# One edit to a one-core transformer kernel: bias tables in four column groups, sums spread between products, first weight units in halves

## What is computed

```python
xn = rms_norm(h, g)                      # before each product; sums of squares over 1024 channels
h = h + rms_norm(ffn, g_ffn_post)        # the end of the first FFN
h = h + sigmoid(h @ w_ple_gate) * e      # starts on the h above, without a norm
bias = rel_bias[t5_bucket(distance)]     # 33 x 16 values, wanted for 1680 distances
logit = q @ k + bias                     # in the last layer, long after the tables are made
```

## Time and profile before

| what | value |
|---|---|
| median of three runs | 1934.17 us (1933.32 to 1936.07) |
| the profiled execution's own time | 1936.29 us |
| its span in the trace | 1934.5 us |
| PE busy | 1891.3 us of it (98%) |
| DVE, ACT, POOL busy | 983.0, 761.2, 763.3 us |
| granted clock of PE, mean | 0.987 of full speed |

### The profile page before, as it was taken

One profiled execution on the slowest core, in us unless ns is written; L12 is line 12 of the kernel. 1 busy time (PEld: TensorE's weight loads), 2 busy tenths in 40 slices (PEclk: granted clock), 3 DMA queues, 4 the chain that ended last, 5 costly groups with the idle time before them and its releaser, 6 DMA issues.

```text
span 1934.5 us, 25284 instructions
## 1 busy us (share of the span) xinstructions
PE 1891.3 (98%) x9354; PEld 1545.6 (80%) x9354; DVE 983.0 (51%) x1639; ACT 761.2 (39%) x1307; POOL 763.3 (39%) x325
## 2 busy tenths in 40 slices
PE   7988999999999999999999999999999999999998
PEld 6886688888888788888888888898866688888886
DVE  6767367643344544235444333743688444344444
ACT  6786544322223351233222222423599642222221
POOL 4323043543444334454445444356300135445452
PEclk9998999999999899999999999999999999999999
DMA  5212032332323223973323333234112023323321
GB/s 190 66 45 66 19 102 69 114 105 87 103 86 103 67 83 108 164 194 100 99 97 97 106 101 95 79 100 136 39 34 67 21 80 118 98 87 97 98 91 62
DMA packets 52238, 177.55 MB, mean 92 GB/s; under 512 B 5527, under 2 KB 5911, under 8 KB 52152
## 3 DMA queue, kind: packets, MB, share of 16 engines
q1 hardware_dynamic: 47952, 166.22, 27.1%
q10 hardware_dynamic: 4200, 10.15, 3.5%
HBM read 166.88 MB, written 9.47 MB: 91 GB/s over the span
## 4 chain that ended last, share of the span: by engine, by line
PE 89%; DVE 6%; ACT 4%; issue 1%; DMA 0%; ACTq 0%; DVEq 0%
PE ps L422 27%; PE ps L423 27%; PE ps L424 27%; PE ps L907 2%; ACT arena L1112 2%; PE ps L893 1%; DVE arena L2263 1%; DVE arena L2240 1%; PE ps L930 1%; DVE arena L1651 1%; ACT arena L1069 1%; PE ps L608 1%; PE ps L574 1%; PE ps L579 1%; PE ps L592 1%
## 5 line engine op out<-in xcount | busy, mean ns | idle before, releaser
L383 POOL TENSOR_TENSOR WL<-raw,WH 128x1024 fp32r<-128x1024 f32 x295 | 736.2, 2510 | 1103.6 <-ACT WH L994 1103.4
L422 PE MATMUL ps<-XH,WH 128*128 128x512 f32 (+1 forms) x1280 | 497.5, 389 | 10.6 <-DMA ident<-in_ident 10.6
L994 ACT ACTIVATE WH<-raw 128x1024 fp32r<-128x1024 f32 x295 | 304.4, 1053 | 509.6 <-PE ps L424 461.0
L423 PE MATMUL ps<-XL,WH 128*128 128x512 f32 (+1 forms) x1280 | 495.8, 387 | 0.0
L424 PE MATMUL ps<-XH,WL 128*128 128x512 f32 (+1 forms) x1280 | 495.6, 387 | 0.0
L422 PE MATMUL ps<-HH,WH 128*128 128x512 f32 x1080 | 423.6, 392 | 5.3 <-DVE XL L1784 4.5
L424 PE MATMUL ps<-HH,WL 128*128 128x512 f32 x1080 | 421.4, 390 | 0.0
L423 PE MATMUL ps<-HL,WH 128*128 128x512 f32 x1080 | 421.2, 390 | 0.0
L422 PEld LDWEIGHTS ps<-XH,WH 128*128 128x128 f32 x1280 | 243.0, 190 | 59.6 <-issue 11.4
L424 PEld LDWEIGHTS ps<-XH,WL 128*128 128x128 f32 x1280 | 242.8, 190 | 48.0
L423 PEld LDWEIGHTS ps<-XL,WH 128*128 128x128 f32 x1280 | 243.0, 190 | 47.2
(11 more groups left out here) (260 smaller groups left out, 1715.0 us busy)
## 6 DMA issues: line engine op xcount, KB each, us to landing
raw<-in_weights SPq DMA_DIRECT2D x301, 512.0 KB, 3.6
tab<-arena ACTq DMA_DIRECT2D x1, 5120.0 KB, 76.7
arena<-tab SPq DMA_DIRECT2D x16, 256.0 KB, 2.9
ftab<-arena ACTq DMA_DIRECT2D x1, 2080.0 KB, 23.4
h<-in_xT SPq DMA_DIRECT2D x8, 256.0 KB, 8.8
out_T<-h SPq DMA_DIRECT2D x8, 256.0 KB, 2.1
arena<-ftab ACTq DMA_DIRECT2D x4, 256.0 KB
arena<-in_pT ACTq DMA_DIRECT2D x1, 512.0 KB, 3.5
```

The lines of the kernel that those rows point to most:

```text
L383: nc.gpsimd.tensor_tensor(WL[:, s, :], raw[:, s, :], WH[:, s, :].bitcast(f32), SUB)\
L422: nc.tensor.matmul(out, wh, xh, start=start, stop=False)
L423: nc.tensor.matmul(out, wh, xl, start=False, stop=False)
L994: nc.scalar.activation(WH[:, s, :], raw[:, s, :], ACT.Copy).then_inc(*m["whi"].tick())
```

## The change

In the opening, units 0 and 1 are loaded, rounded and lowered in halves of 512 columns, the identity comes second on ScalarE's queue, positions and mask are issued after the norm's first part, ScalarE loads its table ahead of the data, and PE runs twelve products of `ones` before `quad`, which no longer waits for `vec` and `ident` itself. At the FFN's opening the sum of squares is cut in three and set between products. At the tables, `spread` comes first, then the four pieces, each into its own 32 columns of the array and its own 32 partitions of one bank, then eight products of the identity. The table rows therefore lie on partitions 0, 32, 64 and 96 onward, and are stored in five transfers in place of two. VectorE's order in the update of h is changed so that XL of a chunk comes one operation earlier.

```diff
         @block.sync
         def _(sp):
-            for c in range(DC):
-                if c in (0, 1, 4, 5):
-                    at = c // 4 * 2 + c % 2
-                    sp.dma_start(raw[:, at, :], io["weights"][SOURCE[at]]).then_inc(raw_in[at], 16)
+            def unit(at, half=None):
+                cols = slice(0, 1024) if half is None else slice(512 * half, 512 * half + 512)
+                sp.dma_start(raw[:, at, cols], io["weights"][SOURCE[at]][:, cols])\
+                  .then_inc(half_in[at] if half == 0 else raw_in[at], 16)
+            def chunk(c):
                 sp.dma_start(h[:, c, :], io["xT"][c * P:(c + 1) * P, :]).then_inc(x_in[c], 16)
+            unit(0, 0)
+            chunk(0)
+            unit(1, 0)
+            chunk(1)
+            unit(0, 1)
+            unit(1, 1)
+            for c in range(2, DC):
+                if c in (4, 5):
+                    unit(c - 2)
+                chunk(c)
...
-            sp.wait_ge(sems["tab_st"], 32)
+            sp.wait_ge(sems["tab_st"], 80)
...
-            for u in range(20):
+            def lower_half(u, half):
+                cols = slice(512 * half, 512 * half + 512)
+                pool.wait_ge(*((sems["whi"], u + 1) if half else (sems["first_hi"], u + 1)))
+                nc.gpsimd.tensor_tensor(WL[:, u, cols], raw[:, u, cols], WH[:, u, cols].bitcast(f32), SUB)\
+                  .then_inc(sems["wlo" if half else "first_lo"], 1)
+            for half in range(2):
+                for u in range(2):
+                    lower_half(u, half)
+            for u in range(2, 20):
...
-                        if c % 4 == 0 and t % 2 == 0:
+                        if halves and c < 4:
+                            if t % 2 == 0 and c % 2 == 0:
+                                pe.wait_ge(sems["wlo" if c else "first_lo"], u + 1)
+                        elif c % 4 == 0 and t % 2 == 0:
...
-            def tables(part):
-                for i in part:
-                    if i == 3:
-                        pe.wait_ge(*m["tab_out"].next())
-                    w = min(S, 1680 - S * i)
-                    nc.tensor.matmul(ps[0:H2, 4 + i % 3, 0:w], relb[0:33, 0:H2], ohs[0:33, S * i:S * i + w],
-                                     start=True, stop=True).then_inc(*m["tab_done"].tick())
+            def tables():
+                pe.wait_ge(sems["onehot_in"], 16)
+                pe.wait_ge(sems["relb_in"], 16)
+                pe.wait_ge(sems["relb_pad"], 1)
+                for i in range(4):
+                    cols, w = piece(i)
+                    last = nc.tensor.matmul(ps[32 * i:32 * i + 32, 4, 0:w], relb[0:33, :], ohs[0:33, cols],
+                                            start=True, stop=True, skip_group_check=True)
+                last.then_inc(*m["tab_done"].tick())
             pe.wait_ge(sems["const_ok"], 2)
-            pe.wait_ge(sems["vec_in"], 16)
-            pe.wait_ge(sems["ident_in"], 16)
-            quad(XH, XL, m["x_lo"], {6: lambda: total(7), 7: spread})
+            for _ in range(12):
+                nc.tensor.matmul(ps[:, 5, 0:P], ones[:, :], ones[:, :], start=True, stop=True)
+            def first_spread():
+                pe.wait_ge(sems["ident_in"], 16)
+                spread()
+            quad(XH, XL, m["x_lo"], {6: lambda: total(7), 7: first_spread}, halves=True)
...
-                total(7, 2)
-            quad(XH, XL, m["x_lo"], {6: ffn_total, 7: spread})
+                total_added(7, 2)
+            quad(XH, XL, m["x_lo"], {6: ffn_total, (6, 2): lambda: total_square(0, 2), (7, 0): lambda: total_square(1, 2),
+                                     (7, 3): spread})
...
-            pe.wait_ge(sems["onehot_in"], 16)
-            pe.wait_ge(sems["relb_in"], 16)
             total(7, 2)
-            tables((0,))
             spread()
-            tables((1, 2, 3))
+            tables()
             pe.wait_ge(*m["tile_free"].upto())
-            keep_busy(5, (b.t + 3) % 4)
+            keep_busy(8, (b.t + 3) % 4)
...
-                        upper((1, 2, 3, 4)[min(c, 3)])
+                        if c < 2:
+                            upper_half(c, 0)
+                        elif c == 2:
+                            upper_half(0, 1)
+                            upper_half(1, 1)
+                        else:
+                            upper(min(c, 4))
...
             act.dma_start(vec[:, :], io["vecs"]).then_inc(sems["vec_in"], 16)
+            act.dma_start(ident[:, :], io["ident"]).then_inc(sems["ident_in"], 16)
+            act.wait_ge(sems["const_ok"], 1)
+            nc.scalar.activation(rstd[:, 0:1], ones[:, 0:1], ACT.Copy).then_inc(sems["warm"], 1)
+            act.wait_ge(sems["vec_in"], 16)
+            split_h("g_mix_pre")
+            upper(6)
             act.dma_start(pos.bitcast(mybir.dt.int32), io["positions"].to_broadcast([P, S]))\
                .then_inc(sems["rope_in"], 16)
             act.dma_start(mask1, io["mask"]).then_inc(sems["mask_in"], 16)
-            act.dma_start(ident[:, :], io["ident"]).then_inc(sems["ident_in"], 16)
-            act.wait_ge(sems["vec_in"], 16)
-            split_h("g_mix_pre")
-            upper(6)
             root(D)
...
-            def copy_table(i):
-                w = min(S, 1680 - S * i)
+            def copy_tables():
                 act.wait_ge(*m["tab_done"].next())
-                nc.scalar.activation(tabs[0:H2, S * i:S * i + w], ps[0:H2, 4 + i % 3, 0:w], ACT.Copy).then_inc(*m["tab_out"].tick())
-            copy_table(0)
+                for i in range(4):
+                    rows, (_, w) = slice(32 * i, 32 * i + 32), piece(i)
+                    nc.scalar.activation(tabs[rows, 0:w], ps[rows, 4, 0:w], ACT.Copy).then_inc(*m["tab_out"].tick())
             for c in range(DC):
                 act.wait_ge(*m["h_upd"].next())
                 nc.scalar.activation(XH[:, c, :], h[:, c, :], ACT.Copy).then_inc(*m["x_hi"].tick())
-                if c < 3:
-                    copy_table(1 + c)
+                if c == 2:
+                    copy_tables()
...
-                    act.dma_start(io["ftab"], tabs[0:H2, 640:].unsqueeze(1).to_broadcast([H2, 32, 1040]))\
-                       .then_inc(sems["tab_st"], 16)
-                    act.dma_start(io["tab"], tabs[0:H2, 0:640].unsqueeze(1).to_broadcast([H2, P, 640]))\
-                       .then_inc(sems["tab_st"], 16)
+                    for to, i, lo, hi in ((0, 1, 128, S), (384, 2, 0, S), (896, 3, 0, 144)):
+                        act.dma_start(io["ftab"][:, :, to:to + hi - lo],
+                                      tabs[32 * i:32 * i + H2, lo:hi].unsqueeze(1).to_broadcast([H2, 32, hi - lo]))\
+                           .then_inc(sems["tab_st"], 16)
+                    for to, i, hi in ((0, 0, S), (S, 1, 128)):
+                        act.dma_start(io["tab"][:, :, to:to + hi],
+                                      tabs[32 * i:32 * i + H2, 0:hi].unsqueeze(1).to_broadcast([H2, P, hi]))\
+                           .then_inc(sems["tab_st"], 16)
...
+            V.memset(relb[0:33, H2:32], 0.0).then_inc(sems["relb_pad"], 1)
...
+            def lower_plain(c):
+                dve.wait_ge(*m["x_hi"].next())
+                V.tensor_tensor(XL[:, c, :], h[:, c, :], XH[:, c, :].bitcast(f32), SUB).then_inc(*m["x_lo"].tick())
+            for c in range(DC):
+                V.scalar_tensor_tensor(Y[:, c, :], Y[:, c, :], col("g_ffn_post", c), root_, MUL, MUL).then_inc(*m["y_tmp"].tick())
                 if c:
-                    dve.wait_ge(*m["x_hi"].next())
-                    V.tensor_tensor(XL[:, c - 1, :], h[:, c - 1, :], XH[:, c - 1, :].bitcast(f32), SUB).then_inc(*m["x_lo"].tick())
+                    lower_plain(c - 1)
+                dve.wait_ge(*m["y_tmp"].upto())
+                V.tensor_tensor(h[:, c, :], h[:, c, :], Y[:, c, :], ADD).then_inc(*m["h_upd"].tick())
+            lower_plain(DC - 1)
```

More of the change, by code:

```diff
@@ L204, in build, with piece @@
         act_, abs_, ay = cut(2564, 2, S), cut(3588, 2, S), cut(4612, 2, S)
-        ohs, relb, tabs, bcs = cut(14352, 1680), cut(16032, H2), cut(8192, 1680), cut(9728, GR, S)
+        ohs, relb, tabs, bcs = cut(14352, 1680), cut(16032, 32), cut(8192, S), cut(9728, GR, S)
+        def piece(i):
+            return slice(S * i, min(1680, S * i + S)), min(S, 1680 - S * i)
         rt, st_ = cut(0, 4, S), cut(2048, 4, S)
@@ L287, in build @@
         x_in = [ctx.enter_context(nc.semaphore(f"x_in{c}")) for c in range(DC)]
+        half_in = [ctx.enter_context(nc.semaphore(f"half_in{s}")) for s in range(2)]
         raw_in = [ctx.enter_context(nc.semaphore(f"raw_in{s}")) for s in range(NSLOT)]
@@ L479, in by_token, with quad @@
                 m["tile_free"].n += TT
-            def quad(xh, xl, x_sem, hooks={}):
+            def quad(xh, xl, x_sem, hooks={}, halves=False):
                 for c in range(DC):
@@ L504, in quad, with total_added @@
                 x_sem.next(DC)
-            def total(n, apart=0):
```

(26 more changed lines are left out.)

13 lines of the change are left out of this document (6 added, 7 removed).

## The result

The changed kernel takes 1963.28 us (median of 4 runs, 1960.25 to 1966.99) against 1935.12 for the kernel before in the same runs (1933.32 to 1937.39): ratio 1.0153, 95% interval 1.0139 to 1.0167. The profiled execution took 1965.29, its span is 1963.5. One of the eleven runs of `spaced` (experiment 4) took 3070.42 us at a mean granted clock of 0.57 and is left out of its ratio.

The account below looks back on a forecast made before the run. The prediction took TensorE (PE), 89% of the chain that ended last, as the bound. 1936.3 (profiled execution) - 5.0 - 2.8 - 2.5 + 40 = 1966; that execution is 2.1 above the median, hence 1964 us, range 1928 to 1974.

Parts of the forecast that it names:

- The opening: At the kernel's start: PE's first product 4.0 us earlier and the clock up before it; gain 5.0, ends 1.5 and 6.2.
- PE now runs ahead of the rest ... 1.1 us late: In the opening: PE outruns POOL's lowerings, with one VectorE operation let in between, so chunk 4's XL comes 1.1 us late.
- The FFN's opening: At the FFN's opening sums: cut in three between products, the clock stays up; gain 2.8, ends 0 and 3.
- The tables: At the tables: spread first, four pieces at once in about 1.7 us; gain 2.5, ends -1.9 and +3.8.
- The stores: At the table stores: weights wait behind the five stores, PE 38 us late plus 2 for low clock; +40.
- q1's silence: Sign around 770 to 840: no q1 packet from the first store until about 835.
- ScalarE's wait on a weight load: Sign around 770 to 840: ScalarE waits on a weight load for some 50 us.
- Three more issues ... cost nothing: At the stores: three more ScalarE issues, 0.65 each, 2 us, delay the rounding by less than its margin.
- the 130: At the stores: a DMA engine's queue holds some 130 packets, so `tab` is handed over only when `ftab` is nearly out.
- The turn by turn rule: At the stores: DMA engines go round robin between queue rows packet by packet; by it the +40 would be zero.
- Weights come through as before: Rival at the stores: weight loads are not held by the new stores; 1924 us, chance 17%.
- The fixed time per row: Rival at the stores: hand-over limited by row count, 7.2 ns each, PE 19 us late; 1945 us, chance 13%.

Follow-up runs that it names:

- `spaced` (experiment 4): The changed kernel with its same five stores, the two tab parts issued one and two loop turns later; 1929.96 us, ratio 0.9982 to the kernel before.
- experiment 8: experiment 1 plus, in the opening, VectorE adding a chunk's squares after the XL of the next chunk; 1928.07 us, ratio 0.9969 to the kernel before.
- `sp_stores`: The same run as experiment 3: the changed kernel with SyncE issuing the five stores; 1971.91 us, ratio 1.0207 to the kernel before.
- experiment 2: The kernel before with only its two table stores cut into five by columns, all from partitions 0 to 15; 1967.79 us, ratio 1.0179.
- experiment 7: A kernel computing nothing: eleven groups of ScalarE stores without loads; the changed kernel's fifth store taken 35.5 us after the first from 16 partitions, 11.0 from 128.
- experiment 6: Two kernels computing nothing: ScalarE stores, each or each group followed by four SyncE unit loads; in six single stores, first dozens of load packets begun after 6.3 to 17.0 us.
- experiment 3: The changed kernel with SyncE issuing the five stores among its weight requests, some 23 us earlier than ScalarE did; 1971.91 us, ratio 1.0207 to the kernel before.
- experiment 1: The changed kernel with table pieces written side by side onto partitions 0 to 15 and the two stores of before; 1930.34 us, ratio 0.9987 to the kernel before.

## Why the prediction was right, and where it was not

The time was right (1964 said, 1963.28 measured), but its closeness is luck: two errors cancelled. I said 10.3 of gains and +40; it was 3.9 and +32.9: 1936.3 - 3.9 + 32.9 = 1965.3, the profiled execution.

- **The opening: said 5.0, measured 1.5.** First product (7.06) and clock came as worked out. The step that failed is "PE now runs ahead of the rest ... 1.1 us late". I let one addition of VectorE in between POOL's lowerings; two stretched operations stood ahead of PE's need, the fourth XL was 2.39 late, where I had the fifth 1.1 late, and the clock fell behind the wait (1.7 more). Without that wait it is 5.1 (experiment 8), near my figure. The opening is touchy: `spaced` and `sp_stores`, whose opening is the changed kernel's, have their first spread at 28.51 and 28.44, where the first addition happened to be short (0.68 in place of 1.78), so the gain of the same program was 1.5 in two profiles and 4.5 in two. The Trainium skill (SBUF — State Buffer, "SBUF: two separate sides") says that VectorE with two SBUF inputs and a GpSimd operation that reads SBUF take turns at a shared port pair, exclusively, for a whole instruction. The trace agrees: 2.89 and 2.84 beside lowerings of 2.6 each, 0.68 and 0.74 without. My sum let this happen once, and it happened twice.
- **Between: 1.0 of these 1.5 lost** by 296 us. At 157 us the lead was whole, at 180 it was 0.7, and in 150:160 the granted clock was 0.76 in place of 0.95. That an earlier fall of the clock took it is a reading that no run here isolates, and 1.0 is no more than executions differ by: this stretch takes 262.3 to 264.1 in the five profiles with the old front half and 262.6 to 264.7 in the six with the new.
- **The FFN's opening: said 2.8, came to 1.0** (0.5 to 1.5 ahead). Full clock came as said, but 0.80 and 0.83 of waits followed. With the spread one tile before the end, VectorE's first operation for the next product was late; that cover I had not looked at. The 1.0 belongs to this pair. From the FFN's first sum to that of the tables the new order takes 349.8 in all six profiles, and the old one 350.8 in two and 349.2 in three, where the spread came 7.0 behind the sum and not 8.2. Against those three the new order loses 0.6.
- **The tables: said 2.5, measured 2.3** (1.5 to 3.9 ahead). Four column groups in 1.74 us. From the first sum to the gate's fourth tile the new order takes 12.1 to 12.2 in all six profiles, the old one 14.5 in two, 12.9 in two and 16.1 in one, so the gain lies between 0.7 and 3.9.
- **The stores: said +40, measured 32.9.** Direction and place were right: the fifth store could not be taken until the fourth was partly out, and PE waited for it once. Two parts of the mechanism were wrong. I had the next store fit when the rows ahead were nearly out; the hold ended with 79 rows per engine left (61 to 88 in most holds, 113 to 114 in some), so the last store was in at 805.5, where I had it fit only near 837. And I had the weights' requests stand behind it; it was ScalarE itself that stood, held at its own issue with four loaded units before it (experiments 2, 4, 7). Of the signs that I had named, q1's silence came (to 822.6, since SyncE had asked for nothing before 809.24), but ScalarE's wait on a weight load was 18 us and not some 50. "Three more issues ... cost nothing" was the sentence that hid this: each was priced at 0.65 us from rows in which only two stores followed each other.
- **What made q1 silent before 793**, the observation from which I drew the 130, is another thing: a load asked for behind a store moves when some 1.3 to 1.6 MB of it have gone (experiment 6). The turn by turn rule of the Trainium skill (DMA: Bandwidth & Descriptors, "Queues, rings and completion order") fits once both move (528 q1 and 711 q10 packets in 824:834), but has no such head start; there the measurement decides.
- **The rivals.** "Weights come through as before" is out: 1963 in place of 1924, and the first unit after the stores was rounded at 827.5. The fixed time per row fits the changed kernel by accident (35.7 us for 3584 rows) and falls in experiment 7, where the same rows took 11.0 us from 128 partitions.

Open: what decides between some 80 rows and some 113; why SyncE's weight request was held 31.6 us in experiment 3, until 41 rows per engine were left; and what holds the third and fourth issue some 4.5 us each. SyncE's fourth request before the change, held 4.54, has the length of these short holds, which come in experiment 7 with no second queue at work. So that hold, from which I drew that a request waits for `tab`, need not have had to do with `tab` at all; no run here tests it.

## What to carry to other kernels

An issue of a transfer is an instruction that can stand, and everything behind it on its engine stands too: price a series of stores by the rows that must leave before the last is taken, not by the length of one issue. Splitting transfers by columns multiplies rows; space them over the work (experiment 4), or write the data so that fewer stores do (experiment 1), or read them from more partitions (experiment 7, so far only on an idle chip). When an edit lets one engine start earlier, look for which engine it now runs into: here the wait cost twice, 2.39 itself and 1.7 in the clock behind it. And before a gain of a microsecond is put down to a part, look how far several profiles of the unchanged program lie apart.

## What the runs showed of the hardware

- Issues of stores by one engine, 512 rows each from 16 partitions: the first two took 0.6 us, the third 4.4 to 4.6 and the fourth, of 512 or 2048 rows, 4.2 to 4.6 (1.4 from 128 partitions; 2.4 and 2.9 with rows of 512 bytes).
- Issues held behind many rows were taken when 61 to 88 rows per DMA engine were left ahead, in four cases 113 to 114, and in experiment 3 a weight request when 41 were. With 2048 rows ahead, read from 16 partitions, even a second issue is held (5.2 us; 18.9 where the rows ahead had 2560 bytes).
- A load behind a store on another queue began after 1.3 to 1.6 MB of it, or when it was nearly out: 14 to 17 us from 16 source partitions, 6.3 from 128.
- Stores that read 16 partitions moved some 90 to 105 GB/s at every row length from 512 to 4160 bytes.
- Four fp32 pieces of 33 rows by 32 columns in four column groups took 1.74 us (1.5 to 1.9 over six profiles), where the three of 512 columns and one of 144 took 5.7 one after another at low clock.
